# Operands and squares from a feature-wise layout in SBUF, in a hybrid MLA, conformer and memory-attention block on one core

## The chip, the core and the metric

The kernel runs on one core of a Trainium2 chip. TensorE (PE) multiplies, VectorE (DVE), ScalarE (ACT) and GpSimd (POOL) work on rows of 128 partitions, SyncE (SP) issues most of the transfers from HBM. The metric is the device time of one execution in microseconds, lower is better. What kernel() does to its inputs on the host before the launch is not in that time.

## The reference, cut to what matters

One layer over 256 tokens of 2048 features, all in float32, with one output. The change touches the three ways in which an input is brought in: x and mem are normalised and multiplied by a weight, and small parameter vectors scale or shift features.

```
h = rms_norm(x, norm_mix);  c_q, c_kv, k_rope, u_in, gate_a, gate_b = split(h @ w_in)
y_a = mla_branch(...)                       # 16 heads, chunk-causal
y_b = conformer_conv_branch(...)            # GLU, causal depthwise conv with 31 taps w_dw, LayerNorm, SiLU, w_pw2
x = x + (sigmoid(gate_a) * y_a + sigmoid(gate_b) * y_b) @ w_o
mem_n = rms_norm(mem, norm_mem)             # 256 memory rows
x = x + memory_cross_attention(rms_norm(x, norm_cross), mem_n, w_q_mem, w_kv_mem, w_o_mem)
x = x + swiglu(rms_norm(x, norm_ffn), w_gate, w_up, w_down);  return rms_norm(x, norm_final)
rms_norm(x, g) = x * rsqrt(mean(x * x) + 1e-6) * g
```

## The kernel before

Every product is made of three: an operand and a weight tile are each split into a high and a low part of type fp32r, and TensorE adds lo x hi, hi x lo and hi x hi into PSUM (`products`, L346 to L348). A weight tile is two 128-row slices of 512 columns (512 KB). It goes through a ring of four slots: SP loads `raw`, ACT copies it to `w_hi` (`split_hi`, L779) once the product four tiles earlier is done, DVE subtracts to `w_lo` (`split_lo`, L1236), and SP may refill `raw` after that. For each tile TensorE makes 12 products, 2 token blocks x 2 slices x 3.

The operand has to stand with its features on the partitions. x and mem lie token-wise in `xs` (two blocks of 128 tokens), so TensorE turns them: `turn_x(g, q)` transposes four 128x128 blocks, that is group g of two feature slices, into the PSUM tile `tp`. ACT scales the group by the gain while it copies it to `mixT[0]` (`x_hi`, L796), DVE subtracts to `mixT[1]` (`x_lo`, L1254), and `products` of tile t read group t.

The program is a hand-written order for each engine, and semaphores join them. The stages of this text, each a run of weight tiles:
- Stage A, tiles 0 to 7: the query latent, x times the first 512 columns of w_in. Groups 0 and 1 are turned ahead, group t + 2 behind tile t. Tile 0 is written out as `head_products` (L382), and `keep_busy(5)` twice (L376) fills TensorE's wait for data with products of the identity; one such float32 product shows as two records. Tiles 8 to 15 are the kv latent and the rope key, 320 columns wide (L444 to L446). Between the two TensorE turns the parameter vectors (L426) and the taps (L429), which POOL's queue has loaded row-wise.
- Stage B, 4 x 8 tiles: the GLU inputs. The last eight run while ACT squares mem for its norm.
- Stage C, 8 passes of 12 tiles: gates, query and key/value of a head pair (L569 to L571, L549 to L551), with the attention of the pair before between them.
- Stage E: keys and values of the memory. Its operand is mem, which POOL's queue has loaded into `xs`. TensorE turns two groups behind tile 8 and two at the end of the last pass of C, two behind tile 2 and two behind tile 4 of E: 32 transposes in four lots of eight.

The sum of squares of a row is taken from `xs` on ACT: a Square with an accumulator over 512 features, and a read of the accumulator (L804), 8 times for x, in A, and 8 times for mem, in B. DVE adds them, POOL takes the power, and the factor scales the results when ACT moves them out of PSUM (L844 in A). ACT frees an accumulator bank (`acc_free`) after that copy and a Square of the same bank.

Of the kernel before, what the change touches and what calls it, by code (L numbers as in the profile page):

```python
# [20 lines left out]
F32 = mybir.dt.float32  # L21
# [43 lines left out]
Q_X, Q_CQ, Q_CKV, Q_B, Q_C, Q_M0, Q_LAST, Q_M1 = 0, 4, 5, 6, 10, 17, 19, 20  # L65
Q_K, Q_D, Q_F, Q_G, Q_H = 22, 26, 30, 31, 35

H_X, H_CQ, H_CKV, H_M0, H_M1, H_D, H_F, H_H = 0, 8, 10, 11, 15, 19, 27, 29
# [3 lines left out]
Z_X, Z_CQ, Z_CKV, Z_MEM, Z_F, Z_H, Z_J = 0, 8, 10, 12, 20, 28, 36  # L72
# [13 lines left out]
def program(nc, x, mem, positions, norm_mix, w_in, b_conv_in, norm_cq, w_uq, norm_ckv, w_ukv, w_dw,  # L86
            b_dw, ln_conv_g, ln_conv_b, w_pw2, b_pw2, w_o, norm_cross, norm_mem, w_q_mem, w_kv_mem,
            w_o_mem, norm_ffn, w_gate, w_up, w_down, norm_final, out):
    def kview(w):
# [5 lines left out]
    mem_v = mem.rearrange("o (b p) d -> (o p) b d", p=P)  # L95
    out_v = out.rearrange("o (b p) d -> (o p) b d", p=P)
    vec_dram = dict(norm_mix=norm_mix, norm_cross=norm_cross, norm_mem=norm_mem, norm_ffn=norm_ffn,
                    b_conv_in=b_conv_in, norm_cq=norm_cq, norm_ckv=norm_ckv, b_dw=b_dw,
                    ln_conv_g=ln_conv_g, ln_conv_b=ln_conv_b)

    ctx = ExitStack()
    with ctx:
# [3 lines left out]
        def sem(name):  # L106
# [4 lines left out]
        vec_rows = sb(ctx, "vec_rows", [P, P])  # L111
# [31 lines left out]

        early = ExitStack()
# [61 lines left out]
        x_head, hi_head, lo_head = sem("x_head"), sem("hi_head"), sem("lo_head")  # L206
        mem_in, x_back, mix_in, vec_in, wdw_in, pos_in, row_in, gain_in = (sem(n) for n in
            ("mem_in", "x_back", "mix_in", "vec_in", "wdw_in", "pos_in", "row_in", "gain_in"))
        ident_made, consts_made, freq_made, zeros_made = (sem(n) for n in
            ("ident_made", "consts_made", "freq_made", "zeros_made"))  # L210
        vec_turned, vec_ready, wdw_turned, wdw_ready = (sem(n) for n in
            ("vec_turned", "vec_ready", "wdw_turned", "wdw_ready"))
# [39 lines left out]
        flat = "p f b j -> p (f b j)"  # L252

# [8 lines left out]
        def _(sp):  # L262
# [9 lines left out]
            def x_piece(lo, hi, done):  # L272

                sp.dma_start(xs[:, :, lo:hi], x_v[:, :, lo:hi]).then_inc(done, 16)

            x_piece(0, TOK, x_head)
            for t in range(16):
                if t in (2, 4, 6):
                    x_piece(t * TOK, (t + 2) * TOK, x_in[t // 2])
                if t < 8:  # L280
                    tile(T_A, t, win_v[:, 2 * t:2 * t + 2, 0:CH], 2, CH)
                else:
                    tile(T_A, t, win_v[:, 2 * t - 16:2 * t - 14, COL_KV:COL_U], 2, COL_U - COL_KV)
                if t == 0:
                    x_piece(TOK, CH, x_in[0])
# [41 lines left out]
        def _(pe):  # L327
# [50 lines left out]
            def head_products():  # L378
# [7 lines left out]
                pe.wait_ge(turned_hi, 1)  # L386
# [4 lines left out]
                pe.wait_ge(turned_out[0], 1)  # L391
# [8 lines left out]
            keep_busy(5)  # L400
            pe.wait_ge(mix_in, 16)
            turn(xt[:, 0:DK], vec_rows[0:DK, :], ident[0:DK, 0:DK]).then_inc(vec_turned, 1)


            def turn_x(g, q):

                turn_group(q, g % 2, [xs[:, b, (2 * g + k) * P:(2 * g + k + 1) * P]
                                      for k in range(2) for b in range(NB)])

            pe.wait_ge(x_head, 16)  # L410
            turn_x(0, 0)
            keep_busy(5)
            pe.wait_ge(x_in[0], 16)
            turn_x(1, 0)
# [12 lines left out]
            pe.wait_ge(wdw_in, 16)  # L427
            for j in range(CT):
                ins = turn(sc[:, 0, 32 * j:32 * j + TAPS], ln_tok[0:TAPS, 0, j * P:(j + 1) * P], ident[0:TAPS, 0:TAPS])  # L429
            ins.then_inc(wdw_turned, 1)  # L430
# [23 lines left out]
            for c in range(4):  # L454
                for t in range(8):
# [7 lines left out]
                    if t == 1 and c > 0:  # L463
                        turn_stage(Q_B + c - 1, 2 * (S_B + c))

# [54 lines left out]
            def gate_and_pair(i, first, last=False):  # L520
# [9 lines left out]
                for t in range(2):  # L530
                    tile_products(i * 12 + T_C, 8 + t, t, 2, cqT, 2 * t, 2, UQ, i * 3 + (C_C + 1))
                    if last and t == 0:

                        turn_x(0, Q_M0)
                        turn_x(1, Q_M0)
                kv_products(i * 12 + T_C, i * 3 + (C_C + 2))
                if last:
                    turn_x(2, Q_M0 + 1)
                    turn_x(3, Q_M0 + 1)
# [43 lines left out]
            for t in range(8):  # L583

                pe.wait_ge(turned_out[t % 2], (Q_M0 + t // 2 if t < 4 else Q_M1 + t // 2 - 2) + 1)
# [4 lines left out]
                if t == 2:  # L590
                    turn_x(4, Q_M1)
                    turn_x(5, Q_M1)
                    attention(2, PAIRS - 1, Q_LAST)
                if t == 4:
                    turn_x(6, Q_M1 + 1)
                    turn_x(7, Q_M1 + 1)
                if t == 5 or t == 7:
# [1309 lines left out]
```

## Time and profile before

| | us |
|---|---|
| median of 3 runs (1680.45 to 1680.94) | 1680.72 |
| the profiled execution | 1680.31 |
| its span, first to last instruction | 1678.5 |
| TensorE busy | 1662.8 |
| VectorE busy | 1091.0 |
| ScalarE busy | 818.9 |

The profiled execution lies 0.4 us under the median, and 1.8 us of it lie outside the span. The page divides the span into 40 slices; TensorE is nine tenths busy or more in all but the last. Records of products overlap, because each is shown with its way through the array: a record of 0.39 us follows the one before it after 0.23 us. So distances are read from start to start.

### The profile page before, as it was taken

To read this page: it belongs to the slowest core of one execution; us is meant where nothing else is said; L and a number is where in the kernel's file an instruction comes from. 1 tells how busy PE (TensorE), PEld (TensorE's weight loads), DVE (VectorE), ACT (ScalarE), POOL (GpSimd) and SP (SyncE) were. 2 spreads that over 40 slices of the span, in tenths; PEclk is the share of its full clock that TensorE was granted. 3 is DMA by queue.
4 is the path that set the end of the run, shared out by engine and by line. 5 is a ranking of instruction groups with operands and counts; after the bars stand their busy time and mean duration, and the time that the engine had idled before them with its cause. 6 is when DMAs were issued, how large, how long until landed. Compare 5 with 4: busy or idle time off the path is not lost.

```text
span 1678.5 us, 23555 instructions
## 1 busy us (share of the span) xinstructions
PE 1662.8 (99%) x7692; PEld 1383.5 (82%) x7692; DVE 1091.0 (65%) x1396; ACT 818.9 (49%) x1053; POOL 108.2 (6%) x160
## 2 busy tenths in 40 slices
PE   9999999999999999999999999999999999999998
PEld 8888888888888888878888788888888888888886
DVE  5555777678887457884448856666666666654453
ACT  7455655555545444555435644444444444344343
POOL 5100100011000000120001200000000000000000
PEclk9999999999999999999999999999999999999999
DMA  7865555555566655554445666666666666565563
GB/s 233 272 193 168 169 164 153 167 158 161 174 210 181 197 187 183 179 194 148 135 137 177 191 196 194 191 190 187 190 199 199 192 196 189 191 221 187 178 214 133
DMA packets 161284, 309.70 MB, mean 185 GB/s; under 512 B 10308, under 2 KB 17074, under 8 KB 160977
## 3 DMA queue, kind: packets, MB, share of 16 engines
q1 hardware_dynamic: 158864, 301.50, 57.8%
q0 software_dynamic: 1776, 6.47, 1.0%
q10 hardware_dynamic: 592, 1.06, 0.2%
q8 instruction: 31, 0.51, 0.1%
q14 instruction: 21, 0.16, 0.0%
HBM read 306.89 MB, written 2.10 MB: 184 GB/s over the span
## 4 chain that ended last, share of the span: by engine, by line
PE 92%; DVE 4%; issue 2%; ACT 1%; DMA 0%; DVEq 0%; SPq 0%; ACTq 0%; POOLq 0%; POOL 0%
PE acc L346 27%; PE acc L348 27%; PE acc L347 27%; DVE w_lo L1236 2%; PE tp L358 2%; DVE x_f L1549 1%; PE sc L675 1%; PE acc L569 1%; PE sc L491 1%; PE acc L571 1%; PE acc L570 1%; ACT w_hi L779 1%; PE acc L549 0%; PE acc L551 0%; PE acc L550 0%
## 5 line engine op out<-in xcount | busy, mean ns | idle before, releaser
L1236 DVE TENSOR_TENSOR w_lo<-raw,w_hi 128x1024 fp32r<-128x1024 f32 (+3 forms) x591 | 718.4, 1221 | 477.2 <-ACT w_hi L779 468.1
L779 ACT ACTIVATE w_hi<-raw 128x1024 fp32r<-128x1024 f32 (+3 forms) x591 | 606.5, 1029 | 767.3 <-PE acc L348 732.1
L346 PE MATMUL acc<-w_hi,crossT 128*128 128x512 f32 x832 | 325.7, 391 | 0.8 <-DVEq L1567 0.8
L348 PE MATMUL acc<-w_hi,crossT 128*128 128x512 f32 x832 | 323.9, 389 | 0.0
L347 PE MATMUL acc<-w_lo,crossT 128*128 128x512 f32 x832 | 323.8, 389 | 0.0
L346 PE MATMUL acc<-w_hi,mixT 128*128 128x512 f32 x796 | 315.5, 396 | 1.2 <-DVEq L1567 0.7
L348 PE MATMUL acc<-w_hi,mixT 128*128 128x512 f32 x796 | 310.5, 390 | 0.0
L347 PE MATMUL acc<-w_lo,mixT 128*128 128x512 f32 x796 | 310.1, 390 | 0.0
L346 PEld LDWEIGHTS acc<-w_hi,crossT 128*128 128x128 f32 x832 | 156.2, 188 | 33.7 <-issue 1.6
L348 PEld LDWEIGHTS acc<-w_hi,crossT 128*128 128x128 f32 x832 | 156.2, 188 | 32.7
L347 PEld LDWEIGHTS acc<-w_lo,crossT 128*128 128x128 f32 x832 | 156.2, 188 | 32.0
L346 PEld LDWEIGHTS acc<-w_hi,mixT 128*128 128x128 f32 x796 | 149.5, 188 | 35.9 <-issue 3.9
L348 PEld LDWEIGHTS acc<-w_hi,mixT 128*128 128x128 f32 x796 | 149.4, 188 | 31.6
L347 PEld LDWEIGHTS acc<-w_lo,mixT 128*128 128x128 f32 x796 | 149.6, 188 | 29.3
L1363 DVE SCALAR_TENSOR_TENSOR conv<-uT,wdwT,conv (+1 forms) x240 | 118.4, 493 | 19.5 <-DVE conv L1363 16.7
L346 PE MATMUL acc<-w_hi,actT 128*128 128x512 f32 x336 | 130.7, 389 | 0.0
L348 PE MATMUL acc<-w_hi,actT 128*128 128x512 f32 x336 | 130.7, 389 | 0.0
L347 PE MATMUL acc<-w_lo,actT 128*128 128x512 f32 x336 | 130.7, 389 | 0.0
L1658 DVE STREAM_TRANSPOSE row_bc<-stage 32x256 f32<-32x256 f32 x176 | 76.7, 436 | 3.6
L347 PEld LDWEIGHTS acc<-w_lo,actT 128*128 128x128 f32 x336 | 63.1, 188 | 13.2
L346 PEld LDWEIGHTS acc<-w_hi,actT 128*128 128x128 f32 x336 | 63.1, 188 | 13.2
L348 PEld LDWEIGHTS acc<-w_hi,actT 128*128 128x128 f32 x336 | 63.1, 188 | 12.9
(244 smaller groups left out, 1350.9 us busy)
## 6 DMA issues: line engine op xcount, KB each, us to landing
raw<-in_w_in_dram SPq DMA_DIRECT2D x104, 512.0 KB, 3.7
raw<-in_w_gate_dram SPq DMA_DIRECT2D x88, 512.0 KB, 4.3
raw<-in_w_up_dram SPq DMA_DIRECT2D x88, 512.0 KB, 3.8
raw<-in_w_down_dram SPq DMA_DIRECT2D x80, 512.0 KB, 3.8
raw<-in_w_kv_mem_dram SPq DMA_DIRECT2D x64, 512.0 KB, 3.9
raw<-in_w_o_dram SPq DMA_DIRECT2D x32, 512.0 KB, 4.0
raw<-in_w_q_mem_dram SPq DMA_DIRECT2D x32, 512.0 KB, 3.7
raw<-in_w_o_mem_dram SPq DMA_DIRECT2D x32, 512.0 KB, 3.9
```

The source lines that it names most:

```text
L346: mm(o, lo, whi, start=first and k == 0, stop=False)
L347: mm(o, hi, wlo, start=False, stop=False)
L348: ins = mm(o, hi, whi, start=False, stop=end)
L358: ins = turn(tp[:, bank, j * P:(j + 1) * P], src, ident[:, :])
L491: mm(sc[:, h, at:at + keys], qnT[:, h, qs:qs + P], knT[:, h, 0:keys], start=qs == 0, stop=False, skip_group_check=True)
L569: mm(o, lo, w_hi[:, s, k * n:(k + 1) * n], start=first and k == 0, stop=False)
L570: mm(o, hi, w_lo[:, s, k * n:(k + 1) * n], start=False, stop=False)
L571: ins = mm(o, hi, w_hi[:, s, k * n:(k + 1) * n], start=False, stop=last and k == kt - 1)
L779: fn(w_hi[:, s, 0:width], raw[:, s, 0:width], ACT.Copy).then_inc(hi_done, 1)
L1236: V.tensor_tensor(w_lo[:, s, 0:width], raw[:, s, 0:width], w_hi[:, s, 0:width].bitcast(F32), ALU.subtract).then_inc(lo_done, 1)
L1363: ins = V.scalar_tensor_tensor(out=a, in0=u, scalar=wt, in1=a, op0=ALU.mult, op1=ALU.add)
L1658: ins = V.transpose(dst[:, :, :, 32 * i:32 * i + 32], src[:, :, :, 32 * j:32 * j + 32])
```

## The change

kernel() lays x, mem, the ten parameter vectors and the taps out with features on the partitions, before the launch. In the program:
- SP loads x feature-wise into the same SBUF (`xs_k`), the first half of the first weight tile ahead of it. POOL's queue loads mem so, and the taps in one transfer. ACT's queue loads all vectors in one transfer.
- `turn_x` is gone, with its 64 transposes, and so are the turns of the vectors and taps (10). ACT makes `mixT[0]` from `xs_k` (`operand_hi`), DVE makes `mixT[1]` (`operand_lo`). For mem, groups 0 to 3 follow tiles 8 to 11 of the last pass of C, groups 4 to 7 follow tiles 0 to 3 of E.
- Squares: ACT squares two slices at a time into `sqT` (`squares`, 8 instructions for each of x and mem, no accumulator). DVE folds 16 slices to 4 in three additions of 1024 elements (`fold_squares`), and TensorE multiplies the folded tile by a column of ones (`add_squares`, 8 products of one column) into PSUM: for x between tiles 6 and 7 of A, for mem behind the last tile of B.
- `keep_busy(17)` stands ahead of tile 0, in place of two times 5.
- x token-wise is still loaded back into `xs` for the residual, as before.

```diff
             def x_piece(lo, hi, done):
-                sp.dma_start(xs[:, :, lo:hi], x_v[:, :, lo:hi]).then_inc(done, 16)
-            x_piece(0, TOK, x_head)
+                sp.dma_start(xs_k[:, lo:hi, :], xT[:, lo:hi, :]).then_inc(done, 16)
+            sp.dma_start(raw[:, 0, 0:CH], win_v[:, 0, 0:CH]).then_inc(raw_head, 16)
+            x_piece(0, 2, x_head)
...
+            def add_squares(n):
+                pe.wait_ge(sq_added, n + 1)
+                for b in range(NB):
+                    for k in range(4):
+                        ins = mm(xt[:, b:b + 1], sqT[:, k, b * P:(b + 1) * P], ones[:, :], start=k == 0, stop=k == 3)
+                ins.then_inc(sq_out, 1)
...
                 else:
-                    pe.wait_ge(turned_out[t % 2], t // 2 + 1)
+                    pe.wait_ge(op_lo, t + 1)
                     products(T_A, t, 8, mixT, 2 * t, 2, CH, C_A)
-                if t + 2 < 8:
-                    if t % 2 == 0:
-                        pe.wait_ge(x_in[t // 2 + 1], 16)
-                    turn_x(t + 2, t // 2 + 1)
-            pe.wait_ge(vec_in, 16 * (len(VECS) - 1))
-            turn(xt[:, P:P + NVEC], vec_rows[0:NVEC, :], ident[0:NVEC, 0:NVEC]).then_inc(vec_turned, 1)
...
+                if t == 6:
+                    add_squares(0)
...
+            def operand_hi(g, name):
+                for k in range(2 * g, 2 * g + 2):
+                    ins = fn(mixT[0][:, k, :], xs_k[:, k, :], ACT.Copy, scale=vcol(name, k))
+                ins.then_inc(op_hi, 1)
+            def squares(g):
+                fn(sqT[:, 2 * g:2 * g + 2, :], xs_k[:, 2 * g:2 * g + 2, :], ACT.Square).then_inc(sq_done, 1)
...
-                    for b in range(NB):
-                        sum_squares(Z_X + 2 * t + b, R_X, b, t, xs[:, b, t * CH:(t + 1) * CH])
+                for g in ((0, 1), (2, 3), (4,), (5,), (6, 7), (), (), ())[t]:
+                    squares(g)
...
+            def fold_squares(n, part):
+                if part == 0:
+                    dve.wait_ge(sq_done, 8 * n + 4)
+                    V.tensor_tensor(sqT[:, 0:4, :], sqT[:, 0:4, :], sqT[:, 4:8, :], ALU.add).then_inc(sums_step, 1)
+                else:
+                    dve.wait_ge(sq_done, 8 * n + 8)
+                    V.tensor_tensor(sqT[:, 8:12, :], sqT[:, 8:12, :], sqT[:, 12:16, :], ALU.add).then_inc(sums_step, 1)
+                sums[0] += 1
+                if part == 1:
+                    dve.wait_ge(sums_step, sums[0])
+                    V.tensor_tensor(sqT[:, 0:4, :], sqT[:, 0:4, :], sqT[:, 8:12, :], ALU.add).then_inc(sq_added, 1)
...
+                if t == 2 or t == 5:
+                    fold_squares(0, t // 4)
+                if t == 6:
+                    mean_of_folded(0, R_X)
```

TensorE at the end of tile 6 and the beginning of tile 7 of A, before (the last three products of tile 6, then tile 7):

```order
L346 MATMUL acc<-w_hi,mixT 128x512
L347 MATMUL acc<-w_lo,mixT 128x512
L348 MATMUL acc<-w_hi,mixT 128x512
L346 MATMUL acc<-w_hi,mixT 128x512 [waits lo_done,turned_out1]
L347 MATMUL acc<-w_lo,mixT 128x512
```

The same place in the changed kernel:

```order
L352 MATMUL acc<-w_lo,mixT 128x512
L353 MATMUL acc<-w_hi,mixT 128x512
L412 MATMUL xt<-ones,sqT 128x1 [waits sq_added]
L412 MATMUL xt<-ones,sqT 128x1 x7
L351 MATMUL acc<-w_hi,mixT 128x512 [waits lo_done,op_lo]
L352 MATMUL acc<-w_lo,mixT 128x512
```

The products with ones and their wait for the folded squares stand between the two tiles now. DVE behind weight tile 7, before (the 640-wide rows are tiles 8 and 9, L1254 between them is the operand of tile 7):

```order
L1236 TENSOR_TENSOR w_lo<-raw,w_hi 128x1024 [waits hi_done]
L1236 TENSOR_TENSOR w_lo<-raw,w_hi 128x640 [waits hi_done]
L1265 TENSOR_REDUCE ssum<-sq 128x2 [waits square_sum]
L1271 TENSOR_SCALAR mean_sq<-ssum 128x2 [waits sums_step]
L1299 TENSOR_SCALAR half_rx<-rfac 128x2 [waits r_ready]
L1254 SCALAR_TENSOR_TENSOR mixT<-tp,vecT,mixT 128x256 [waits turned_hi]
L1254 SCALAR_TENSOR_TENSOR mixT<-tp,vecT,mixT 128x256
L1236 TENSOR_TENSOR w_lo<-raw,w_hi 128x640 [waits hi_done] x4
```

The same in the changed kernel:

```order
L1217 TENSOR_TENSOR w_lo<-raw,w_hi 128x1024 [waits hi_done]
L1217 TENSOR_TENSOR w_lo<-raw,w_hi 128x640 [waits hi_done]
L1262 SCALAR_TENSOR_TENSOR mixT<-xs,vecT,mixT 128x256 [waits op_hi]
L1262 SCALAR_TENSOR_TENSOR mixT<-xs,vecT,mixT 128x256
L1217 TENSOR_TENSOR w_lo<-raw,w_hi 128x640 [waits hi_done]
L1273 TENSOR_TENSOR sqT<-sqT 128x1024 [waits sq_done]
L1277 TENSOR_TENSOR sqT<-sqT 128x1024 [waits sums_step]
L1217 TENSOR_TENSOR w_lo<-raw,w_hi 128x640 [waits hi_done]
L1282 TENSOR_SCALAR mean_sq<-xt 128x2 [waits sq_out]
```

The reduction of the sums was ahead of the operand of tile 7; two of the three folds stand behind it now, and behind weight tile 9. On ACT, in that part of the changed kernel, the order is weight tile 7, weight tile 8, the last two squares, the operand of tile 7, weight tile 9. TensorE at the end of C, before (key/value products, then the first tile of E):

```order
L550 MATMUL acc<-w_lo,ckvT 128x512
L551 MATMUL acc<-w_hi,ckvT 128x512
L358 MATMUL tp<-ident,xs 128x128 [waits turned_out0]
L358 MATMUL tp<-ident,xs 128x128 x3
L358 MATMUL tp<-ident,xs 128x128 [waits turned_out1]
L346 MATMUL acc<-w_hi,mixT 128x512 [waits acc_free0,lo_done,turned_out0]
L347 MATMUL acc<-w_lo,mixT 128x512
```

The same in the changed kernel:

```order
L537 MATMUL acc<-w_hi,ckvT 128x512
L538 MATMUL acc<-w_lo,ckvT 128x512
L539 MATMUL acc<-w_hi,ckvT 128x512
L351 MATMUL acc<-w_hi,mixT 128x512 [waits acc_free0,lo_done,op_lo]
L352 MATMUL acc<-w_lo,mixT 128x512
```

Here only the lot of eight transposes is gone, and the first product waits for the same bank.

## Rows read from the trace of the kernel before

**Rows 1.** Page, parts 1, 2 and 4: busy time, granted clock, chain by engine.
```profile
PE 1662.8 (99%) x7692; PEld 1383.5 (82%) x7692; DVE 1091.0 (65%) x1396; ACT 818.9 (49%) x1053; POOL 108.2 (6%) x160
...
PEclk9999999999999999999999999999999999999999
...
PE 92%; DVE 4%; issue 2%; ACT 1%; DMA 0%; DVEq 0%; SPq 0%; ACTq 0%; POOLq 0%; POOL 0%
```

**Rows 2.** TensorE's waits: who for whom, us in total, times, longest.
```profile
PE acc L346 <- DVEq L1567: 2.1, 4, 0.7
...
PE acc L549 <- ACTq L960: 0.3, 1, 0.3
```

**Rows 3.** Timeline, start of the program, TensorE: start, duration, instruction, count, idle before.
```profile
1.53 2.50 PE L376 MATMUL ov<-ident 128*128 128x128 f32 x10 [1.53 <-POOL ident L1727]
...
5.08 1.65 PE L376 MATMUL ov<-ident 128*128 128x128 f32 x10
...
7.69 2.08 PE L382 MATMUL acc<-w_hi,mixT 128*128 128x512 f32 x8
...
14.42 0.50 PE L346 MATMUL acc<-w_hi,mixT 128*128 128x512 f32 x1
```

**Rows 4.** Timeline, start of the program, ACT: weight tile 2.
```profile
11.26 1.06 ACT L779 ACTIVATE w_hi<-raw 128x1024 fp32r<-128x1024 f32 x1 [1.50 <-DMA raw<-in_w_in_dram]
```

**Rows 5.** Timeline, TensorE, tiles 5, 6 and 7 of A, first products.
```profile
24.06 0.48 PE L346 MATMUL acc<-w_hi,mixT 128*128 128x512 f32 x1
...
26.92 0.60 PE L358 MATMUL tp<-ident,xs 128*128 128x128 f32 x4
27.27 0.48 PE L346 MATMUL acc<-w_hi,mixT 128*128 128x512 f32 x1
...
30.28 0.50 PE L346 MATMUL acc<-w_hi,mixT 128*128 128x512 f32 x1
```

**Rows 6.** Timeline, ACT, second half of A.
```profile
22.06 1.06 ACT L779 ACTIVATE w_hi<-raw 128x1024 fp32r<-128x1024 f32 x1
23.01 0.62 ACT L804 ACTIVATE junk<-xs 128x512 f32<-128x512 f32 x1
23.53 0.20 ACT L804 ACTIVATION_READ_ACCUMULATOR junk<-xs 128x1 f32 x1
...
24.39 0.82 ACT L796 ACTIVATE mixT<-tp,vecT 128x256 fp32r<-128x256 f32 x2
25.10 1.68 ACT L779 ACTIVATE w_hi<-raw 128x1024 fp32r<-128x1024 f32 x2
...
32.36 0.69 ACT L844 ACTIVATE stage<-acc,rfac 128x512 f32<-128x512 f32 x1 [1.26 <-PE acc L348]
```

**Rows 7.** Timeline, DVE, end of A.
```profile
23.15 1.23 DVE L1236 TENSOR_TENSOR w_lo<-raw,w_hi 128x1024 fp32r<-128x1024 f32 x1
...
29.36 0.87 DVE L1254 SCALAR_TENSOR_TENSOR mixT<-tp,vecT,mixT 128x256 fp32r<-128x256 f32 x2
30.14 0.81 DVE L1236 TENSOR_TENSOR w_lo<-raw,w_hi 128x640 fp32r<-128x640 f32 x1
```

**Rows 8.** Timeline, TensorE, between tiles 7 and 8 of A.
```profile
33.33 0.67 PE L429 MATMUL sc<-ident,ln_tok 31*128 31x31 f32 x8
33.94 0.41 PE L444 MATMUL acc<-w_hi,mixT 128*128 128x320 f32 x1
...
35.29 0.42 PE L444 MATMUL acc<-w_hi,mixT 128*128 128x320 f32 x1 [0.22 <-ACTq L847]
```

**Rows 9.** Timeline, TensorE, end of the last pass of C.
```profile
402.94 0.61 PE L515 MATMUL ov<-kv_tok,probsT 128*128 128x128 f32 x4
403.39 0.39 PE L512 MATMUL ov<-kv_tok,probsT 128*128 128x128 f32 x2
...
406.17 1.03 PE L358 MATMUL tp<-ident,xs 128*128 128x128 f32 x8
406.96 0.42 PE L569 MATMUL acc<-w_hi,cqT 128*128 128x384 f32 x1
...
409.61 0.47 PE L549 MATMUL acc<-w_hi,ckvT 128*128 128x512 f32 x1 [0.29 <-ACTq L960]
...
412.44 1.03 PE L358 MATMUL tp<-ident,xs 128*128 128x128 f32 x8
```

**Rows 10.** Timeline, ACT, same place: copies of keys and values out.
```profile
411.34 0.69 ACT L966 ACTIVATE kv_tok<-acc,rfac 128x512 f32<-128x512 f32 x1
```

More of the change, by code:

```diff
@@ L110, in program @@
         ident = sb(ctx, "ident", [P, P])
-        vec_rows = sb(ctx, "vec_rows", [P, P])
+        ones = sb(ctx, "ones", [P, 1])
         vecT = sb(ctx, "vecT", [P, NVEC])
@@ L399, in _ @@
             pe.wait_ge(ident_made, 2)
[L400 to L414, printed above, removed]
+            keep_busy(17)
+            def add_squares(n):
[4 more added lines that the diff above has]
+                ins.then_inc(sq_out, 1)
+            pe.wait_ge(consts_made, 2)
             for t in range(8):
@@ L464, in _ @@
                         turn_stage(Q_B + c - 1, 2 * (S_B + c))
+                    if t == 7 and c == 3:
+                        add_squares(1)
             def attention(t, p, q):
@@ L823, in _ @@
             load_table(ACT.Square)
-            act.wait_ge(vec_ready, 1)
-            def x_hi(g, name, count):
-                turned_hi_part(g % 2, count, [mixT[0][:, 2 * g + k, :] for k in range(2)],
-                               gain=[vcol(name, 2 * g + k) for k in range(2)])
-            x_hi(0, "norm_mix", 1)
+            act.wait_ge(vec_in, 16)
+            def operand_hi(g, name):
[4 more added lines that the diff above has]
+                fn(sqT[:, 2 * g:2 * g + 2, :], xs_k[:, 2 * g:2 * g + 2, :], ACT.Square).then_inc(sq_done, 1)
+            act.wait_ge(x_head, 16)
+            operand_hi(0, "norm_mix")
+            act.wait_ge(raw_head, 16)
+            fn(w_hi[:, 0, 0:CH], raw[:, 0, 0:CH], ACT.Copy).then_inc(hi_head, 1)
             act.wait_ge(raw_full[0], 16)
-            fn(w_hi[:, 0, 0:CH], raw[:, 0, 0:CH], ACT.Copy).then_inc(hi_head, 1)
             fn(w_hi[:, 0, CH:TW], raw[:, 0, CH:TW], ACT.Copy).then_inc(hi_done, 1)
-            x_hi(1, "norm_mix", 2)
+            act.wait_ge(x_in[0], 16)
+            operand_hi(1, "norm_mix")
             split_hi(T_A, 1)
@@ L862, in _ @@
                 if t == 2:
-                    act.wait_ge(vec_ready, 2)
                     for g in range(2):
@@ L914, in _ @@
                             act.wait_ge(mem_in, 64)
-                        for b in range(NB):
-                            sum_squares(Z_MEM + 2 * t + b, R_MEM, b, t, xs[:, b, t * CH:(t + 1) * CH])
+                            act.wait_ge(sq_out, 1)
+                        for g in (2 * t, 2 * t + 1):
+                            squares(g)
             def attention(t, p, q):
@@ L1271, in mean_square, with operand_lo, mean_of_folded @@
                 V.tensor_scalar(mean_sq[:, norm, :], src, 1.0 / n, EPS, ALU.mult, ALU.add).then_inc(ms_ready, 1)
[L1274 to L1283 removed]
+            dve.wait_ge(vec_in, 16)
+            def operand_lo(g, name, count):
+                dve.wait_ge(op_hi, count)
+                for k in range(2 * g, 2 * g + 2):
+                    ins = V.scalar_tensor_tensor(out=mixT[1][:, k, :], in0=xs_k[:, k, :], scalar=vcol(name, k),
+                                                 in1=mixT[0][:, k, :].bitcast(F32), op0=ALU.mult, op1=ALU.subtract)
+                ins.then_inc(op_lo, 1)
+            def fold_squares(n, part):
[9 more added lines that the diff above has]
+                    V.tensor_tensor(sqT[:, 0:4, :], sqT[:, 0:4, :], sqT[:, 8:12, :], ALU.add).then_inc(sq_added, 1)
+            def mean_of_folded(n, norm):
+                dve.wait_ge(sq_out, n + 1)
+                V.tensor_scalar(mean_sq[:, norm, :], xt[:, 0:NB], 1.0 / D, EPS, ALU.mult, ALU.add).then_inc(ms_ready, 1)
+            operand_lo(0, "norm_mix", 1)
             for done, ready, half in ((hi_head, lo_head, slice(0, CH)), (hi_done, lo_done, slice(CH, TW))):
@@ L1405, in gate_and_pair @@
                     split_lo(i * 12 + T_C, t + 4, width)
+                    if first and t == 1:
+                        mean_of_folded(1, R_MEM)
                     if first and t == 3:
@@ L1729, in _ @@
             G.memset(minus_half[:, :], -0.5).then_inc(consts_made, 1)
+            G.memset(ones[:, :], 1.0).then_inc(consts_made, 1)
             for j in range(ROPE // 2):
```

165 lines of the change are left out of this document (64 added, 101 removed).

## The prediction

> **What bounds the kernel now.** I read the busy times first: TensorE is busy for 1662.8 of 1678.5 us, DVE for 65%, ACT for 49%, and the chain that ended last lies on TensorE for 92% [rows 1]. Then its waits: one entry of 2.1 us in four pieces, the rest smaller [rows 2]. So TensorE's queue is the time. Whatever leaves it counts in full, unless a wait of TensorE takes its place; what only ACT, DVE or a transfer gains counts nothing. Hence the question at each edit: what does TensorE do less, and is the next thing it needs there in time? This differs by stage, and I read the timeline of three places: the start, the end of A, the end of C.
>
> **The start.** Before, tile 2 of A starts at 14.42 [rows 3]. Ahead of it lie the filler products, tile 0 from 7.69 and two groups of transposes. Now TensorE runs 17 filler products, 34 records, from 1.53. In the trace the first ten records take 2.50 us and the second ten 1.65 [rows 3], 0.24 and about 0.15 from start to start. The granted clock reads nine tenths or more in every slice [rows 1], its level of 2.4 GHz, so that row doesn't explain the slower ten. All 34 at the slow pace end at 9.8, all at the fast one at 6.7; I take 7.5, the slow pace for the first 4 us and a little better than 0.15 after. Twelve products at 0.23 make tile 0 end at 10.3. But tile 1 and 2 don't wait for TensorE: weight tile 2 was copied at 11.26, and ACT had idled for 1.50 until its transfer landed [rows 4]. The same bytes go in the same order now, so it lands about then, or up to 0.5 earlier since the pieces are longer. Behind it come ACT's copy (0.95 from start to start [rows 6]), ACT's operand of tile 2 (0.66; from PSUM 24.39 to 25.10, 0.71 [rows 6]) and, behind its w_lo, DVE's operand (0.79 from start to start [rows 7]). The longer way is DVE's: 11.0 + 0.95 + 0.15 for the hand-over, w_lo 1.14 (the 1.23 row less its overlap), operand 0.79: 14.0, and I take 13.9. Bounds: 13.1, where only TensorE limits, and 15.2, with the fillers at their slow pace. Against 14.42: **-0.5** (-1.3 to +0.8).
>
> **Tiles 2 to 6.** From tile 5 to 6, with a group of transposes, 3.21 us pass; from 6 to 7, without one, 3.01, of which some 0.2 are a wait for the operand of tile 7 that DVE finished at 30.23 [rows 5, 7]. So a tile is 2.78 and a group 0.43. Four such groups between tile 2 and 6 are gone, and a fifth behind tile 5, 5 x 0.43, and the 0.2: **-2.35**. Other engines keep up: per tile ACT has 0.95 + 0.66 + at most 2 x 0.52 = 2.65 against 2.78, DVE 1.14 + 0.79. Tile 6 would end at 13.9 + 5 x 2.78 = 27.8.
>
> **The wait for the folded squares.** In front of tile 7 TensorE now waits for three engines' work. The last squares stand on ACT behind weight tile 8, whose slot comes free when tile 4 is done, at 13.9 + 3 x 2.78 = 22.2. From there: hand-over 0.2, the narrow copy at 0.63 (the row of a wide and a narrow one is 1.68, less 0.95, less 0.1 that overlaps with the next), two squares at 0.52, the operand of tile 7 at 0.66, weight tile 9 at 0.63 [rows 6]. DVE's operand of tile 7 ends near 26.4, w_lo of tile 9 takes 0.73 to 27.2, and two dependent additions of 1024 elements, at the price of w_lo of the same size, 1.14 and 1.23 [rows 7], end at 29.6. So TensorE waits 29.7 - 27.8 = **+1.9**. The lower bound needs no ACT backlog at all: weight tile 9 can't be copied before tile 5 is done, and 0.2 + 0.63 + 0.73 + 2.4 + 0.2 behind that is 1.4 after the end of tile 6. The upper one, folds at 1.5 each, is 2.6. Queued behind the waiting TensorE is all of tile 7; behind DVE's folds w_lo of tile 10, which is not needed for three tiles.
>
> **The products with ones.** 8 float32 products, 16 records, of one column. No row has one column. The nearest: transposes of 31 x 31 at 0.61 / 8 = 0.076 [rows 8], and float32 records of 128 columns with a full weight load at 0.45 / 4 = 0.112 [rows 9]. One column streams less than either, but loads 128 x 128 like the second. I take 0.09 between them, 16 x 0.09 = **+1.45**; bounds 1.0 and 1.8.
>
> **Tile 8 of A.** The 9 transposes of vectors and taps are gone from between tile 7 and 8, and I cost that at **nothing**. The second half of tile 8 started at 35.29, released by ACT's Square of the accumulator [rows 8], a chain that starts with ACT's copy at 32.36 [rows 6], hangs on tile 7 and is not changed: 5.01 us after tile 7's start either way. The transposes lay under that wait. The factor for this copy comes 1.3 us behind the products with ones, by 2.08 needed. Sum of A: -0.5 - 2.35 + 1.9 + 1.45 = **+0.5**.
>
> **End of B.** The other products with ones, **+1.45**, are pure addition. Here they stand behind the last tile, and the folds behind the ninth: by the same chain, with wide tiles, 4.9 us behind the end of tile 5 against 5.56 for tiles 6 and 7. No wait, or up to 0.5. ACT saves eight accumulator reads, which nobody waits for.
>
> **Memory operand.** A lot of eight transposes delays the next product by 406.96 - 406.17 = 0.79 and costs some 0.08 at the restart: 0.87, four times 3.5 [rows 9]. Two of four are partly taken back. Behind the first, TensorE waited 0.3 for ACT's copy of the queries anyway [rows 2, 9]; behind the second, the first tile of E needs the bank that ACT's copy of the keys and values empties, from 411.34 for 0.69 [rows 10], which now also stands behind one operand more. I follow the two copies and get 1.3 for the first two lots in place of 1.74, and 1.74 for the others, within E: **-3.0** (-3.5 to -2.3). DVE has four operand steps in the first four tiles of E in place of two double ones; its total is the same.
>
> **A rule against the change.** ACT reads x from SBUF where it read PSUM. In the trace a Square of 512 from SBUF takes 0.62 and a copy of 512 out of PSUM 0.69 [rows 6]; I expect no loss. The Trainium skill, "VectorE: DVE Perf Modes", section "The TRN2 errata — SBUF-src ops pay a fixed extra latency per instruction", says the opposite for ScalarE: 224 cycles against 172 from PSUM, 43 ns more an instruction at its 1.2 GHz. The trace's rows disagree with it. By it, an estimate, the wait for the folds would be 0.1 to 0.2 longer, which changes no other number.
>
> **The sum.** +0.5 + 1.45 - 3.0 = -1.05 us. The profiled execution had 1680.31 and lies 0.4 under the median; the difference applies to either, and from the median, 1680.72, it gives **1679.7 us**. A change within 0.2%, 3.4 us, is what a measurement of this kernel can hardly tell from none.
>
> **The rivals.**
> *All transposes gain, folds hidden.* If the start is limited by TensorE alone (-0.8 more), the wait is at its lower bound (-0.5), both sets of ones cost 1.0 (-0.9) and the memory lots count in full (-0.5), it is -3.7: 1677.0. For it: TensorE is the bound nearly everywhere. Against: the 1.4 us of wait are in the order of the program.
> *TensorE slows down after the wait.* Slower than before: 1.9 us of standing still and 1.45 of one-column work could let its clock fall to its lower level, 1.2 GHz, as the start had records at 0.24 in place of 0.15 or less [rows 3]. At half rate a tile costs 2.78 more. Falls at both products with ones, for one tile each, give 5.6 - 1.05 = +4.5: 1685.2. It turns the result when more than 1.05 us is lost, and passes 0.2% when 4.4 is. Against: the granted clock never fell in a slice, through TensorE's waits before [rows 1, 2], though none was longer than 0.7.
> *ACT is late at every tile of A*: it has only 0.13 a tile to spare. Each tile then takes 3.0, the transposes' 0.43 is given back by half, and A ends 5 x 0.22 = 1.1 later: 1680.8. Against: before it did 3.1 us of work a tile there (0.95 + 0.71 + 2 x 0.72 from start to start [rows 6]), and does less now.
>
> **How the numbers follow.** Chances: forecast 0.70 (1678.0 to 1681.3), ACT late 0.13, everything gains 0.11, slower clock 0.06. The range of eight in ten takes in the faster case and the upper bounds of the forecast (fillers slow +1.3, ones 0.7, folds 0.7, not all at once): 1677.0 to 1682.4. Faster by over 0.2% needs 1677.4 or less, 0.10; slower needs 1684.1, 0.05; within 0.85.
>
> **What would show it.** In the changed profile: tile 2 of A between 13.1 and 14.5; a wait of TensorE on DVE's fold, 1.4 to 2.6 us, its longest; tile 7 starting at 30.3 to 31.5; 16 records with ones in 1.0 to 1.8 us; tile 8's second half again 5.0 behind tile 7's start; between the end of B's last tile and the first product of C 1.0 to 2.0; the first tile of E 1.0 to 1.8 nearer to tile 8 of the last pass of C. I am wrong if TensorE doesn't wait for the folds, if a record with ones takes over 0.15, or if products anywhere behind A have a spacing other than 0.23.

## The result and the profile after

The changed kernel takes **1685.36 us** (median of ten runs, 1683.63 to 1686.05) against 1680.85 for the kernel before in the same session (ten runs, 1680.45 to 1681.88): a ratio of 1.0024, 95% interval 1.0015 to 1.0033. It is 4.5 us slower, where 1.0 us of gain was predicted, and it lies above the predicted range. The profiled execution took 1685.06 with a span of 1683.3; before it was 1680.31 and 1678.5. The span grew by 4.8.

The page of the changed kernel, busy times, granted clock and chain by engine, to be held against [rows 1]:

```profile
PE 1663.1 (99%) x7664; PEld 1383.2 (82%) x7664; DVE 1097.2 (65%) x1398; ACT 816.0 (48%) x1037; POOL 102.6 (6%) x152
...
PEclk9999999999999999999999999999999999999999
...
PE 90%; DVE 4%; issue 2%; ACT 2%; DMA 0%; SPq 0%; DVEq 0%; ACTq 0%; POOLq 0%; POOL 0%
```

TensorE has 28 records fewer, 64 + 10 transposes having gone and 32 + 14 records having come, and yet 0.3 us more busy time. Products that run at half rate look like this: fewer records, the same busy time. The clock row is the same as before in every digit, and it hides the cause, as the finer views below show. TensorE's waits (who for whom, us in total, times, longest), against [rows 2]:

```profile
PE acc L351 <- DVEq L1560: 2.2, 4, 0.7
PE xt L412 <- DVE sqT L1277: 2.1, 1, 2.1
...
PE acc L351 <- DVE w_lo L1217: 1.7, 1, 1.7
...
PE acc L437 <- ACTq L838: 0.6, 1, 0.6
PE acc L537 <- ACTq L947: 0.5, 1, 0.5
```

Two large waits are new: for the last fold, and, at the start, for the low part of weight tile 1. Now TensorE's timeline from the start to tile 8 of A (start, duration, instruction, count, idle before), against [rows 3, 5, 8]:

```profile
1.53 5.80 PE L381 MATMUL ov<-ident 128*128 128x128 f32 x34 [1.53 <-POOL ident L1720]
7.09 2.08 PE L387 MATMUL acc<-w_hi,mixT 128*128 128x512 f32 x8
...
15.19 0.50 PE L351 MATMUL acc<-w_hi,mixT 128*128 128x512 f32 x1 [0.47 <-DVE mixT L1262]
...
26.44 0.39 PE L351 MATMUL acc<-w_hi,mixT 128*128 128x512 f32 x1
...
31.45 2.63 PE L412 MATMUL xt<-ones,sqT 128*128 128x1 f32 x16 [2.13 <-DVE sqT L1277]
33.94 0.77 PE L351 MATMUL acc<-w_hi,mixT 128*128 128x512 f32 x1
34.51 0.63 PE L352 MATMUL acc<-w_lo,mixT 128*128 128x512 f32 x1
34.94 0.63 PE L353 MATMUL acc<-w_hi,mixT 128*128 128x512 f32 x1
...
40.90 0.42 PE L437 MATMUL acc<-w_hi,mixT 128*128 128x320 f32 x1 [0.59 <-ACTq L838]
```

Read the distances from start to start. In tile 7 one product of 512 columns follows the other after 0.43 us, where in the tiles before it is 0.23. The granted clock in stretches of 2 us (busy time of PE, PEld, DVE, ACT and POOL, then the clock, the DMA share and GB/s) names the reason:

```profile
30.00:32.00 2.00, 0.55 (x5) 0.55 (x5) 1.97 (x3) 0.16 (x1) 0.00 (x0) 1.00 0.59 170
32.00:34.00 2.00, 2.00 (x14) 2.00 (x13) 0.13 (x1) 0.00 (x0) 0.00 (x0) 0.63 0.32 67
34.00:36.00 2.00, 2.00 (x6) 1.61 (x6) 0.16 (x1) 0.00 (x0) 0.73 (x1) 0.50 0.27 97
36.00:38.00 2.00, 2.00 (x6) 1.52 (x6) 0.00 (x0) 1.05 (x2) 0.00 (x0) 0.50 0.00 0
38.00:40.00 2.00, 2.00 (x9) 1.71 (x8) 0.00 (x0) 0.85 (x3) 0.00 (x0) 0.66 0.00 0
...
146.00:148.00 2.00, 2.00 (x20) 1.92 (x18) 0.96 (x1) 1.31 (x2) 0.00 (x0) 1.00 0.33 125
```

1.00 is 2.4 GHz and 0.50 is 1.2 GHz. The clock falls during the products with ones, 1.1 us after they begin and 3.4 us after tile 6 ended, and is back 6.8 us later (a mean of 0.63 over two microseconds puts the fall at 32.5, the 0.66 puts the return at 39.4). A slice of the page is 42 us wide: 6.8 us at half clock leave 0.92 in it, which still prints as 9. The last line is the other place with products of ones, the end of B, and there the clock stays at 1.00.

The span's 4.8 us, read as the lag of the changed kernel behind the one before at eight points of TensorE's timeline (us):

| point on TensorE | before | after | lag | this step | predicted |
|---|---|---|---|---|---|
| tile 2 of A starts | 14.42 | 15.19 | +0.77 | +0.77 | -0.5 |
| tile 6 ends | 30.11 | 29.16 | -0.95 | -1.72 | -2.15 |
| first product with ones | | 31.45 | | wait, +2.29 | +1.9 |
| tile 7 starts | 30.28 | 33.94 | +3.66 | ones, +2.49; a wait of 0.17 ahead of tile 7 gone | +1.45; -0.2 |
| second half of tile 8 starts | 35.29 | 40.90 | +5.61 | +1.95 | 0 |
| first product of C | 140.69 | 148.00 | +7.31 | ones, +1.70 | +1.45 |
| tile 8 of the last pass of C | 403.98 | 411.66 | +7.68 | +0.37 not assigned | 0 |
| end of the span | 1678.5 | 1683.3 | +4.8 | -2.9 | -3.0 |

"Tile 6 ends" is its last product's start plus 0.23. The two points of the kernel before that no row has shown yet, the last product of tile 6 and the first of C:

```profile
29.88 0.39 PE L348 MATMUL acc<-w_hi,mixT 128*128 128x512 f32 x1
...
140.69 0.39 PE L346 MATMUL acc<-w_hi,mixT 128*128 128x512 f32 x1
```

### The profile page after: what moved, and what is told of

It is laid out like the page before. It is cut to its first block, busy times and chain, and to the rows that moved or that the text cites. A ratio compares the mean times of both kernels' runs of the same rounds, so it can differ in the third digit from the quotient of the medians.

```text
span 1683.3 us, 23466 instructions
## 1 busy us (share of the span) xinstructions
PE 1663.1 (99%) x7664; PEld 1383.2 (82%) x7664; DVE 1097.2 (65%) x1398; ACT 816.0 (48%) x1037; POOL 102.6 (6%) x152
## 4 chain that ended last, share of the span: by engine, by line
PE 90%; DVE 4%; issue 2%; ACT 2%; DMA 0%; SPq 0%; DVEq 0%; ACTq 0%; POOLq 0%; POOL 0%
PE acc L351 27%; PE acc L353 27%; PE acc L352 27%; DVE w_lo L1217 2%; PE tp L363 1%; DVE x_f L1542 1%; ACT w_hi L759 1%; PE sc L655 1%; PE acc L557 1%; PE acc L559 1%; PE sc L486 1%; PE acc L558 1%; DMA raw<-in_w_in_dram 0%; PE ov L510 0%; PE xt L675 0%
```

## The experiments

Every kernel is the changed one with the edit shown.

**1. Fill the wait.** If the low clock is what costs, and not the folds themselves, work that has no use should make the kernel faster. Nine float32 products of the identity stand where TensorE waited.

```diff
                 if t == 6:
+                    keep_busy(9)
                     add_squares(0)
```

> The changed kernel with nine products of the identity (18 records, some 2.05 us) on TensorE between tile 6 of A and its wait for the folded squares. The wait ends at the same moment, since ACT and DVE are untouched; only TensorE no longer stands still in it. Theory 'clock': the loss is the lower clock (0.50 from 32.5 to 39.2 us) that follows the standstill. Then the granted clock stays at 1.00, the 16 one-column records take 1.7 us as they did at the end of B, tile 7 takes 2.8 in place of 5.3, and the second half of tile 8 starts at 38.2 in place of 40.9: 2.7 us faster than the changed kernel, 1682.5. Theory 'wait': the standstill itself and the products are the loss and the clock is beside the point: 1685.3, as the changed kernel.

Measured: 1682.32 us (1681.42 to 1683.49), ratio to the kernel before 1.0011 (1.0001 to 1.0021), 3.0 us less than the changed kernel (2.6, if each is taken by what it has over the kernel before in its own session). TensorE's timeline, and two stretches of the clock:

```profile
29.34 2.17 PE L381 MATMUL ov<-ident 128*128 128x128 f32 x18
31.63 1.95 PE L412 MATMUL xt<-ones,sqT 128*128 128x1 f32 x16
...
38.10 0.41 PE L438 MATMUL acc<-w_hi,mixT 128*128 128x320 f32 x1 [0.28 <-ACTq L839]
```

```profile
32.00:34.00 2.00, 2.00 (x18) 1.91 (x18) 0.47 (x2) 0.00 (x0) 0.14 (x1) 1.00 0.18 30
34.00:36.00 2.00, 2.00 (x10) 1.68 (x9) 0.00 (x0) 0.84 (x2) 0.59 (x1) 1.00 0.38 134
```

The products with ones start as late as before (31.63 against 31.45), since DVE is as late. But the clock stays at 1.00, and the second half of tile 8 starts 2.8 us earlier. So some 2.6 to 3.0 of the 4.5 us are the slow clock, and filling the wait, which doesn't shorten it, takes them back. The one-column work alone, which is still there, doesn't bring the clock down in this profile. Nor is the filling a full cure, it seems: three of the ten executions took 1683.25 to 1683.49, two of them at a mean clock of 0.997, which no execution of experiments 3 and 4 shows (0.998 or 0.999). No profile was taken of these.

**2. The wait alone.** Is the standstill enough by itself? The wait stays between tiles 6 and 7, and the products with ones go behind tile 7.

```diff
                 if t == 6:
+                    pe.wait_ge(sq_added, 1)
+                if t == 7:
                     add_squares(0)
```

> The changed kernel with TensorE's wait for the folded squares where it is, and the products with ones moved behind tile 7. It tells whether the standstill of 2.3 us alone brings the clock down or only together with the one-column products. If the standstill alone does: tile 7 starts at 31.5 and takes up to 5.3 us, the second half of tile 8 starts past 42, 1686 to 1688. If both are needed: tile 7 takes 2.8, the products end at 36.0, the factor is ready at 37.3, the second half of tile 8 starts near 40.1 and the clock reads 1.00 in A: 1684.3.

Measured: 1686.34 us (1685.59 to 1686.64), ratio 1.0032 (1.0020 to 1.0043). TensorE's timeline and clock:

```profile
31.67 0.50 PE L351 MATMUL acc<-w_hi,mixT 128*128 128x512 f32 x1 [2.13 <-DVE sqT L1279]
...
34.52 1.84 PE L412 MATMUL xt<-ones,sqT 128*128 128x1 f32 x16
38.96 0.61 PE L439 MATMUL acc<-w_hi,mixT 128*128 128x320 f32 x1 [2.60 <-ACTq L840]
```

```profile
34.00:36.00 2.00, 2.00 (x18) 1.88 (x17) 0.00 (x0) 0.00 (x0) 0.00 (x0) 1.00 0.38 134
36.00:38.00 2.00, 0.36 (x4) 0.28 (x3) 0.16 (x1) 0.59 (x1) 0.73 (x1) 0.95 0.00 0
38.00:40.00 2.00, 1.04 (x4) 1.07 (x5) 0.00 (x0) 1.87 (x5) 0.00 (x0) 0.50 0.00 0
```

After the same standstill, followed by tile 7, the clock stays at 1.00 through that tile. It falls near 37.8: the ones at 34.52 are now followed by a new wait of 2.60, for the bank that ACT can't free until the factor is there, and the factor comes from the products with ones. So I had moved the ones to a place with a worse wait. The time lies in the range that was expected if the standstill alone sufficed (1686 to 1688), but not for that reason: the standstill between the tiles left the clock at 1.00.

That doesn't mean that a fall needs the products with ones. At the end of the program TensorE has nothing more to do, and the clock falls there too. The last product of the kernel before, and two stretches behind it, then the same of experiment 5 (below):

```profile
1669.74 0.39 PE L755 MATMUL acc<-w_hi,actT 128*128 128x512 f32 x1
...
1672.00:1674.00 2.00, 0.00 (x0) 0.00 (x0) 1.21 (x3) 1.22 (x2) 0.55 (x1) 1.00 0.00 0
1674.00:1676.00 2.00, 0.00 (x0) 0.00 (x0) 0.00 (x0) 0.12 (x1) 0.00 (x0) 0.74 0.92 358
```

```profile
1673.64 0.39 PE L732 MATMUL acc<-w_hi,actT 128*128 128x512 f32 x1
...
1676.00:1678.00 2.00, 0.00 (x0) 0.00 (x0) 1.15 (x2) 1.32 (x2) 0.55 (x1) 0.52 0.00 0
```

Read like the falls above, the clock falls 5.0 us after the last product in the one and 2.2 in the other; in all ten kernels of this text it is 2.2 to 5.4. So standing still is enough if it lasts, and after the same length the clock may or may not have fallen: 2.3 us between two tiles had no effect here, 2.2 at the end of experiment 5 did. What the places in A with a fall share is 4 to 4.8 us from the end of one tile to the start of the next, made of a standstill of over 2 us and 1.7 us or more of one-column products, in either order. Whether one-column products count as work for the clock at all, these runs don't separate.

**3. No folds for x.** What does the wait cost together with the clock? DVE folds nothing, and the products with ones read the first four slices as soon as they are squared. The norm of x is then that of a quarter of the features, so part of the computation is left out.

```diff
             def add_squares(n):
-                pe.wait_ge(sq_added, n + 1)
+                if n == 0:
+                    pe.wait_ge(sq_done, 2)
+                else:
+                    pe.wait_ge(sq_added, n)
...
-                if t == 2 or t == 5:
-                    fold_squares(0, t // 4)
```

> The changed kernel without the three folds of x's squares: the products with ones read the first four slices only, so x's norm is of a quarter of the features (that part of the computation is left out). No wait at tile 6. Theory 'wait and clock': products with ones at 29.2, tile 7 at 30.9, clock 1.00, second half of tile 8 at 35.9 in place of 40.9: 5.0 us faster than the changed kernel, 1680.3. A theory by which the loss lies elsewhere (operands from SBUF, transfers) expects less than 1 us.

Measured: 1679.20 us (1678.74 to 1679.77), ratio 0.9993 (0.9983 to 1.0002).

```profile
28.77 1.84 PE L415 MATMUL xt<-ones,sqT 128*128 128x1 f32 x16
...
35.15 0.42 PE L440 MATMUL acc<-w_hi,mixT 128*128 128x320 f32 x1 [0.27 <-ACTq L841]
```

The products with ones start at 28.77 behind tile 6 with no wait, and the second half of tile 8 starts at 35.15, where the changed kernel has 40.90. Wait and clock together were worth 6.2 us (5.7, by what each has over the kernel before in its own session), more than the whole loss. The rest of the change gains some 1 us, which isn't clear of noise.

**4. The squares ahead.** Can the folds be kept and the wait not? ACT squares the last slices ahead of weight tile 8, which has to wait for tile 4 anyway. DVE makes the last two folds ahead of weight tiles 8 and 9.

```diff
                 for ahead in range(t + 3 if t < 5 else t + 4, t + 4 if t < 4 else t + 5):
+                    if ahead == 8:
+                        squares(6)
+                        squares(7)
                     split_hi(T_A, ahead, TW if ahead < 8 else 2 * (COL_U - COL_KV))
-                for g in ((0, 1), (2, 3), (4,), (5,), (6, 7), (), (), ())[t]:
+                for g in ((0, 1), (2, 3), (4,), (5,), (), (), (), ())[t]:
...
-                for ahead in range(t + 3 if t < 5 else t + 4, t + 4 if t < 4 else t + 5):
+                for ahead in (7,) if t == 4 else (8, 9) if t == 5 else \
+                        range(t + 3 if t < 5 else t + 4, t + 4 if t < 4 else t + 5):
                     split_lo(T_A, ahead, TW if ahead < 8 or ahead >= 16 else 2 * (COL_U - COL_KV))
-                if t == 2 or t == 5:
+                if t == 2 or t == 4:
                     fold_squares(0, t // 4)
```

> The changed kernel, complete, with another order on two engines: ACT makes the last two squares of x ahead of weight tile 8, DVE folds them ahead of the operand of tile 7 and of w_lo of tiles 8 and 9. Squares done at 25.9, second fold done at 28.9, before tile 6 ends at 29.2. Theory 'wait and clock': no standstill, tile 7 at 30.9, clock 1.00, second half of tile 8 at 35.9: 1680.3, the time of the kernel before. [...]

Measured: 1680.35 us (1679.48 to 1680.79), ratio 0.9998 (0.9988 to 1.0007), 5.0 us less than the changed kernel (4.5, each against its own session), and 2.0 less than experiment 1, which has the wait but not the slow clock:

```profile
29.34 1.84 PE L412 MATMUL xt<-ones,sqT 128*128 128x1 f32 x16
...
36.02 0.41 PE L437 MATMUL acc<-w_hi,mixT 128*128 128x320 f32 x1 [0.28 <-ACTq L838]
```

```profile
30.00:32.00 2.00, 2.00 (x15) 1.86 (x15) 2.00 (x3) 0.34 (x1) 0.00 (x0) 1.00 0.12 13
```

No wait ahead of the products with ones, and the clock stays at 1.00. The loss hung on the order of a few instructions on two engines, neither of which bounds the kernel. The prediction had the wait as given by the order of the program; it is, and the order can be changed.

**5 to 7. Why the start is late.** Weight tile 2 is copied at 11.96 where it was 11.26 [rows 4], on ACT:

```profile
11.96 1.06 ACT L759 ACTIVATE w_hi<-raw 128x1024 fp32r<-128x1024 f32 x1 [1.59 <-DMA raw<-in_w_in_dram]
```

It is a transfer that is late, not an engine. Three differences of the first transfers were undone one at a time; these three have no interval. The first has the old order: x's first piece, then the whole of weight tile 0.

```diff
-            sp.dma_start(raw[:, 0, 0:CH], win_v[:, 0, 0:CH]).then_inc(raw_head, 16)
             x_piece(0, 2, x_head)
...
-                if t == 0:
-                    sp.dma_start(raw[:, 0, CH:TW], win_v[:, 1, 0:CH]).then_inc(raw_full[0], 16)
-                elif t < 8:
+                if t < 8:
```

> The changed kernel with the first transfers in the order and size of before: x's first piece, then weight tile 0 whole. Open is why weight tile 2 landed at 11.96 where it landed at 11.26 before, with the same bytes ahead of it. If it is the split and the order of weight tile 0, ACT's copy of tile 2 starts near 11.3 and tile 2 of A near 14.5 (15.19 in the changed kernel). If it is the transfer of all vectors from ACT's queue, it stays near 12.0 and 15.2.

Measured: the copy at 12.09, 1684.1 us. The second leaves only 16 columns of the vectors ahead of everything; the rest come later through POOL's queue.

```diff
-            act.dma_start(vecT[:, :], vecs).then_inc(vec_in, 16)
+            act.dma_start(vecT[:, 0:DK], vecs[:, 0:DK]).then_inc(vec_in, 16)
...
             gp.wait_ge(tile_done, 1)
+            gp.dma_start(vecT[:, DK:], vecs[:, DK:]).then_inc(vec_late, 16)
```

> The changed kernel with only the 16 columns of the first gain in the first vector transfer, and the other 94 columns loaded by POOL's queue once tile 0 is done. If the 128 pieces of 440 bytes hold up the weight tiles, ACT's copy of tile 2 starts near 11.4 and tile 2 of A near 14.6. If the number of pieces (still 128, of 64 bytes) is what costs, it stays at 12.0 and 15.2.

Measured: the copy at 12.04, 1683.7 us. The third lays x out in HBM slice by slice, so that its pieces are 1 KB.

```diff
-                sp.dma_start(xs_k[:, lo:hi, :], xT[:, lo:hi, :]).then_inc(done, 16)
+                sp.dma_start(xs_k[:, lo:hi, :], xT[lo:hi].rearrange("k p n -> p k n")).then_inc(done, 16)
...
-    laid["xT"] = _feature_major(inputs["x"])
+    laid["xT"] = _feature_major(inputs["x"]).transpose(1, 0, 2)
```

> x is laid out slice by slice in HBM, so that its transfers arrive in pieces of 1 KB a partition (before: 1 to 2 KB), where the changed kernel has 2 to 4 KB; nothing else differs. If the long pieces make weight tile 2 land late, ACT copies it at 11.3 to 11.5 in place of 11.96 and tile 2 of A starts near 14.6, with 1684.7 in all. If not, the copy stays at 11.9 to 12.1 and the time at 1684 to 1686, and the lateness has another cause (the vectors' 128 pieces, or the lane over which the pieces are spread).

Measured: the copy at 11.79, 1683.6 us. None brings back 11.26, and none can be told from no effect: in experiments 1 to 4, whose first transfers are those of the changed kernel, the copy starts at 12.14, 12.18, 11.79 and 12.13. (The profile before is a single one, so its own scatter isn't known.) What the windows do show is where the bytes are missed. Between 3 and 4 us the changed kernel moves more, 317 GB/s against 185; then, in the three microseconds from 4 to 7, it moves 173, 217 and 281 against 263, 345 and 401; from 8 us on both move 340 or more. What holds them back there stays open. One difference that wasn't tried is the number of packets on ACT's queue in the first 14 us, 416 against 304.

The same three kernels tell something else. They have the same wait (2.08 to 2.13), but their clock falls later, after the products with ones have run at full pace (16 records in 1.95 us) and some 1 us into tile 7, and it is back after some 3.4 us in place of 6.8. In the first of them:

```profile
32.00:34.00 2.00, 2.00 (x17) 1.92 (x17) 0.42 (x2) 0.00 (x0) 0.19 (x1) 1.00 0.28 49
34.00:36.00 2.00, 2.00 (x7) 1.57 (x6) 0.00 (x0) 0.37 (x1) 0.54 (x1) 0.56 0.32 115
36.00:38.00 2.00, 2.00 (x7) 1.57 (x7) 0.00 (x0) 1.00 (x4) 0.00 (x0) 0.58 0.00 0
38.00:40.00 2.00, 1.39 (x10) 1.13 (x8) 0.00 (x0) 1.82 (x4) 0.00 (x0) 1.00 0.00 0
```

Its second half of tile 8 starts at 39.45, against 40.90. So the same wait gives falls of different length. That fits the spread of the changed kernel's own runs, 1683.6 to 1686.1, with the longer ones at the lower mean clock (0.998 to 0.995).

**8. A version that beats both.** The reordering of experiment 4 and the later vectors. Besides, DVE folds mem's squares further, from four slices to one, by two more additions of 512 and 256 elements. TensorE then needs two products with ones for mem in place of eight, behind tile 2 of the first pass of C. The lines shown are those of this last part.

```diff
             def add_squares(n):
                 pe.wait_ge(sq_added, n + 1)
+                last = 3 if n == 0 else 0
                 for b in range(NB):
-                    for k in range(4):
-                        ins = mm(xt[:, b:b + 1], sqT[:, k, b * P:(b + 1) * P], ones[:, :], start=k == 0, stop=k == 3)
+                    for k in range(last + 1):
+                        ins = mm(xt[:, b:b + 1], sqT[:, k, b * P:(b + 1) * P], ones[:, :], start=k == 0, stop=k == last)
...
-                    if t == 7 and c == 3:
-                        add_squares(1)
...
+                    if first and t == 2:
+                        add_squares(1)
...
+                if n == 1 and part == 1:
+                    sums[0] += 1
+                    for half in (2, 1):
+                        dve.wait_ge(sums_step, sums[0])
+                        ins = V.tensor_tensor(sqT[:, 0:half, :], sqT[:, 0:half, :], sqT[:, half:2 * half, :], ALU.add)
```

> A version that should beat both: the order of e4, the vector transfer of e6, and for mem's squares two more folds (512 and 256 elements) on DVE, two products with ones in place of eight, moved from the end of B to behind tile 2 of C, where nobody needs the factor yet. From 1680.3: up to 0.7 less for the start, 6 x 0.21 = 1.3 less for the products: 1678.3, 2.5 us under the kernel before. If the clock falls anyway at tile 7, 1681 or more.

Measured: 1678.66 us (1678.19 to 1679.20, eleven runs), ratio to the kernel before 0.9988 (0.9979 to 0.9997). TensorE at both places:

```profile
28.99 1.84 PE L413 MATMUL xt<-ones,sqT 128*128 128x1 f32 x16
...
150.35 0.50 PE L413 MATMUL xt<-ones,sqT 128*128 128x1 f32 x4
150.71 0.49 PE L351 MATMUL acc<-w_hi,mixT 128*128 128x512 f32 x1
```

The products for mem now take 150.71 - 150.35 = 0.36 of TensorE's time in place of 1.70, and the additions lie on DVE, which has room. The later vectors gained nothing that can be seen: weight tile 2 is copied at 11.79, as in experiment 3 without them. It is 6.7 us faster than the changed kernel and 2.1 faster than the one before: the transposes are gone, as the prediction had it, and neither a wait for the folds nor the slow clock takes the gain back.

## Why the prediction was wrong

**What bounds the kernel** was read rightly: whatever TensorE spends counts in full.

**The wait for the folds** was the strongest step. It was traced through three engines to +1.9 with bounds 1.4 and 2.6, and measured +2.29. The chain ended as described: DVE's two dependent additions at 28.92 and 30.17, 1.22 and 1.23 long, released TensorE at 31.45.

```profile
28.92 1.22 DVE L1273 TENSOR_TENSOR sqT<-sqT 128x1024 f32<-128x1024 f32 x1
30.17 1.23 DVE L1277 TENSOR_TENSOR sqT<-sqT 128x1024 f32<-128x1024 f32 x1
```

**The step that failed** is what follows that wait. The forecast added it and the products with ones as if TensorE came back at the pace at which it had left. "TensorE slows down after the wait" was written down as a rival, with the right level, and got 0.06. Its counter-argument was "the granted clock never fell in a slice, through TensorE's waits before". That rests on rows that can't bear it in two ways. The slices are 42 us wide, and the changed kernel's row reads all nines too, with the clock at half for 6.8 us. And between the first product and the last no wait before was longer than 0.7, so nothing there spoke of one of 1.9. The one longer standstill in that trace, behind the last product, ends in a fall, which only the finer windows show. A case that the trace doesn't cover is not a case that it speaks against. The price was in its favour as well: it was the only rival that could cost several microseconds.

**The rival's own price** was off. It had the fall at both places with ones, for one tile each, at 5.6 us. It came at one place only. There it cost 0.79 in the products with ones (2.49 against 1.70 from start to start) and 1.95 up to the second half of tile 8, 2.7 in all; by experiment 1, 2.6 to 3.0 in the medians. Tile 7 itself took 2.4 longer, but 0.45 of that was hidden, since behind it TensorE waits for ACT to free a bank. At the end of B no wait stands ahead of the ones, and the clock stayed at 1.00. The rival's total, 1685.2, is near the measured one only because the fall was costed too high and other terms too low.

**Terms that were mis-sized**, without the clock (3.1 us in sum, more than the clock's 2.7):
- The start: +0.77 in place of -0.5, 1.3 off. The step "the same bytes go in the same order now, so it lands about then" failed, weight tile 2 landing 0.7 later. The filler products mattered as little as was said: tile 0 starts at 7.09 against 7.5 predicted (6.73 to 8.09 in the kernels with the same start), and tile 1 waits for its weights either way.
- Tiles 2 to 6: the prediction took out five groups of transposes. Between the start of tile 2 and that of tile 6 there are four (behind tiles 2 to 5), and the prediction counted the one behind tile 5 a second time. From tile 2 to tile 6 TensorE saved (27.27 - 14.42) - (26.44 - 15.19) = 1.60, or 4 x 0.40. With 0.12 in tile 6 and 0.17 of wait ahead of tile 7 it is 1.9 against 2.35. The prediction's own clock times would have told: it has tile 6 end at 27.8, 2.3 before 30.11, where its terms add up to 2.65.
- A product with ones: 1.70 / 16 = 0.106 us a record, not 0.09. The nearest row was the one with the same full weight load (0.112), and from 128 columns to one the cost hardly falls. Twice +0.25.
- ACT's operand from SBUF: two take 0.80 from start to start where the prediction has 0.66, and from PSUM 0.71 before [rows 6]. It lies on the chain of the folds and makes part of the wait's 0.4.

Wait, start, tiles and ones are off by 0.39 + 1.27 + 0.46 + 0.50 = 2.6 together; with 0.1 in the memory operand and the 0.4 in B and C that isn't assigned it is 3.1. Without the fall of the clock the kernel would have ended 2.1 us above the one before, which is 1682.8 from the median of 1680.72, just outside the range; experiment 1 measures that case at 1.95 above. With the clock's 2.7 it is the 4.8 us of the profile. So the sizes alone had turned the forecast gain into a loss, with 1.3 us at the start as the largest of them, and the clock more than doubled it.

**What was right**: memory operand -2.9 (-3.0 predicted); ACT not late in A; tile 8 little changed by the transposes that went (where the clock stays up its second half starts 4.98 behind tile 7 in experiment 4 and 4.66 in experiment 1, against 5.01); no wait at the end of B.

**The rule on operands from SBUF.** The prediction held the Trainium skill, "VectorE: DVE Perf Modes", section "The TRN2 errata — SBUF-src ops pay a fixed extra latency per instruction", to be contradicted by the trace. It isn't. The rows it was weighed by were two different operations, a Square from SBUF and a copy out of PSUM, so that their difference showed the operation as much as the source. The same operation on the same width now stands from both sources, ACT's scaled copies of 256 elements in the changed kernel:

```profile
26.46 0.89 ACT L809 ACTIVATE mixT<-xs,vecT 128x256 fp32r<-128x256 f32 x2
27.26 0.72 ACT L759 ACTIVATE w_hi<-raw 128x640 fp32r<-128x640 f32 x1
```

0.80 for two against 0.71 is 45 ns more for each, and that page of the Trainium skill gives 43.

## What to carry to other kernels

At each new wait of the engine that bounds the kernel, ask what it does right before and right behind, and look at the granted clock there in windows of 2 us, never in the page's slices: a standstill of 2 us beside 2 us of one-column products cost some 3 us more than itself here. If a reduction feeds a step in the middle of a dense run, put its last links (here two squares and two additions) ahead of work that has to wait anyway; where that can't be done, products without use in the wait are better than the wait.

## What the hardware showed that I had not expected

- The clock fell to 0.50 with a standstill of 2.3 us ahead of one-column products (the fall 3.4 us after the last tile), and after one-column products with a standstill of 2.6 behind them; not with the 2.3 us alone between two tiles, nor with 1.7 us of one-column products alone between two tiles. Behind the last product of the program it fell after 2.2 to 5.4 us of standing still alone. It stayed low for 3.4 to 6.8 us in A, although TensorE had dense products again 1.4 us after the fall or sooner; in experiments 5, 6 and 8 it fell only when they were already running. At 0.50 products of 512 columns follow each other after 0.427 us, as the Trainium skill, "TensorE: Matmul & The Clock Gate", section "Wait — 56ns, not 53.3ns?", has it for the lower clock (426.7 ns). At 1.00 these fp32r products took 0.227, where that page of the Trainium skill has 0.216.
- A float32 product of one column costs two records of 0.106 us (0.09 where only four stood together, in the last version): a column of ones is a dear way to add up on the engine that bounds the kernel. Six of eight such products went for two short additions on DVE.
- With features on the partitions, weight tile 2 was copied at 11.79 to 12.18 in nine kernels, against 11.26 token-wise, and the first transfers moved fewer bytes between 4 and 7 us. Undoing the order, the vectors' bytes or the length of the pieces, one at a time, didn't change it visibly.
